# Weight preparation moved to other products of the feed-forward, query/key and shared-key stages, and three broadcasts of norm factors one product later

## The reference

```python
# end of the first block: feed-forward, then the final norm
h = rms_norm(x, norm2_g)
f = jnp.square(jax.nn.relu(h @ w_ff1))        # 1024 -> 4096
x = x + f @ w_ff2                             # 4096 -> 1024
x = rms_norm(x, final_g)
# second block, layer A
h = _rms(x, a_norm)
q, k, v, g = jnp.split(h @ a_w_in, 4, axis=-1)   # queries and keys get an own norm per head and a rotation
...                                              # differential attention
x = x + o @ a_w_out
# layer B: keys and values first
kv = _rms(x, kv_norm) @ w_kv
...                                              # stick-breaking attention, second output projection
```

## Time and profile before

| | |
|---|---|
| median of 3 runs | 2633.3 us (2632.38 to 2633.53) |
| the profiled execution | 2640.83 us, its span 2639.0 us |
| PE busy | 2385.6 us, 90% of the span |
| DVE busy | 1543.8 us, 58% |
| ACT busy | 955.1 us, 36% |
| POOL busy | 209.3 us, 8% |
| mean granted TensorE clock | 0.946 |
| DMA | 115.99 MB, mean 44 GB/s |

### The profile page before, as it was taken

How to read it: one execution, slowest core, us unless ns; L and a number is a source line. 1 busy time by engine, 2 the same in 40 slices (tenths; PEclk the granted TensorE clock), 3 DMA queues, 4 the chain that set the end, 5 groups by cost and what they waited for, 6 DMA issues and landing times.

```text
span 2639.0 us, 30077 instructions
## 1 busy us (share of the span) xinstructions
PE 2385.6 (90%) x12784; PEld 1263.2 (48%) x12784; DVE 1543.8 (58%) x1979; ACT 955.1 (36%) x1346; POOL 209.3 (8%) x264
## 2 busy tenths in 40 slices
PE   6997759999999999769999877899999998988899
PEld 3443324444444444334444445664444446776664
DVE  5579885565444555576741388975524405878852
ACT  5232233322121221323321276752212214777741
POOL 0000002000000000333310201013000000000000
PEclk9997879999999999889999989999999996889999
DMA  4010000120101101012010000012120100000021
GB/s 169 32 64 32 32 0 1 64 96 33 64 32 64 64 33 64 33 34 96 33 64 32 33 1 1 1 68 93 50 110 33 65 0 33 1 1 1 1 81 48
DMA packets 50321, 115.99 MB, mean 44 GB/s; under 512 B 2384, under 2 KB 7817, under 8 KB 49804
## 3 DMA queue, kind: packets, MB, share of 16 engines
q1 hardware_dynamic: 48452, 105.39, 11.2%
q10 hardware_dynamic: 1736, 8.68, 0.8%
HBM read 101.49 MB, written 12.58 MB: 43 GB/s over the span
## 4 chain that ended last, share of the span: by engine, by line
PE 66%; DVE 20%; ACT 8%; issue 4%; DMA 1%; POOL 1%; ACTq 0%; DVEq 0%; POOLq 0%
PE PS L72 62%; DVE R L101 7%; ACT RG L81 5%; PE PS L75 4%; DVE RG L101 2%; DVE R L93 2%; DVE mx L110 2%; DVE RG L107 2%; DVE scl L110 2%; ACT R L81 1%; ACT OV L84 1%; POOL R L93 1%; DVE RG L93 1%; DVE oss L110 0%; DVE mx L96 0%
## 5 line engine op out<-in xcount | busy, mean ns | idle before, releaser
L72 PE MATMUL PS<-R,RG 128*128 128x512 f16 (+1 forms) x5472 | 1179.2, 377 | 44.6 <-DVE R L101 29.8
L72 PEld LDWEIGHTS PS<-R,RG 128*128 128x128 f16 (+1 forms) x5472 | 545.7, 104 | 675.0 <-issue 65.7
L72 PE MATMUL PS<-RG,R 128*128 128x512 f16 x2880 | 631.6, 379 | 3.8 <-DVE R L101 3.8
L72 PEld LDWEIGHTS PS<-RG,R 128*128 128x128 f16 x2880 | 281.9, 98 | 335.7 <-DVE R L101 4.2
L81 ACT ACTIVATE R<-PS,scl 128x512 f32<-128x512 f32 (+1 forms) x200 | 131.2, 686 | 724.6 <-PE PS L72 576.7
L72 PE MATMUL PS<-R,OV 128*128 128x64 f32 (+2 forms) x1456 | 205.2, 296 | 58.2 <-DVE R L93 30.9
L101 DVE SCALAR_TENSOR_TENSOR R<-PS,scl,R 128x512 f32<-128x512 f32 (+1 forms) x216 | 154.9, 746 | 173.6 <-PE PS L72 124.9
L107 DVE TENSOR_TENSOR_SCAN RG<-RG 128x127 f32<-128x127 f32 (+7 forms) x128 | 168.6, 1345 | 120.9 <-ACT RG L81 120.5
L101 DVE SCALAR_TENSOR_TENSOR RG<-RG,scl 128x4096 f16<-128x4096 f32 x42 | 188.6, 4491 | 77.2 <-ACT RG L81 77.2
L72 PEld LDWEIGHTS PS<-R,OV 128*128 128x128 f32 x1456 | 192.1, 210 | 69.3 <-DVE R L93 37.3
L81 ACT ACTIVATE RG<-RG,scl 128x4096 f16<-128x4096 f32 x42 | 155.7, 3708 | 141.9 <-DVE scl L113 141.9
(11 more groups left out here) (109 smaller groups left out, 1536.7 us busy)
## 6 DMA issues: line engine op xcount, KB each, us to landing
RG<-in_w_ff SPq DMA_DIRECT2D x16, 2048.0 KB, 8.1
RG<-in_a_w_in SPq DMA_DIRECT2D x8, 2048.0 KB, 8.6
RG<-in_w_in SPq DMA_DIRECT2D x4, 2048.0 KB, 9.9
xspill<-R ACTq DMA_DIRECT2D x2, 4096.0 KB, 11.7
RG<-in_w_kv SPq DMA_DIRECT2D x4, 2048.0 KB, 8.4
RG<-in_b_w_in SPq DMA_DIRECT2D x4, 2048.0 KB, 7.9
R<-in_x SPq DMA_DIRECT2D x8, 512.0 KB, 9.2
RG<-in_w_out SPq DMA_DIRECT2D x2, 2048.0 KB, 7.8
```

Source lines behind the costliest of these rows:

```text
L72: return self.engine.matmul(*a, **k) if self.engine else Nothing()
```

## The change

Three things are moved; no operation is added or taken away, apart from `final_x` being issued in two halves of four k.

- Tables: tile 22 is measured at use 6 of tile 19 (before: use 1 of tile 20), with factor and high half at use 1 of tile 20 (before 2) and low half at use 2 (before 3). Tile 23 is measured at use 7 of tile 20 (before: use 1 of tile 21). Tile 24 is measured at use 2 of tile 23, u = 5 (before u = 0), converted at u = 6 and 7 (before u = 1 and 2). Tile 25 is measured at use 7 of tile 22, u = 10 (before u = 4); its conversion stays at u = 12 and 13. Tile 33 keeps its measure (use 4 of tile 31) and is converted at uses 4 and 5 of tile 32 (before: uses 5 and 6 of tile 31). Tile 34 is measured at use 8 of tile 32 and converted at uses 1 and 2 of tile 33 (before: uses 1, 2 and 3 of tile 32). Tile 35 is measured at use 5 of tile 33 and converted at uses 6 and 7 (before 1, 2 and 3).
- Half 0 of the final norm: spread at j = 8, `final_h` at j = 8 to 11, the second diagonal at j = 11, its spread at j = 12, `final_x` at j = 12 and 13.
- Half 1: the second diagonal at u = 4, its spread at u = 6, `final_x` at u = 6 and 7, the spill at u = 9.

```diff
-for _i, _at in ((21, 9), (23, 5), (35, 8)):
-    del CONVERT[_i, 2]
-    CONVERT[_i, _at] = _i + 2
-del MEASURE[35, 1]
-MEASURE[35, 3] = 37
-for _i in (7, 8, 30, 31):
+for _i in (7, 8, 19, 20, 21, 22, 23, 30, 31, 32, 33, 35):
     del MEASURE[_i, 1], CONVERT[_i, 2]
-CONVERT[6, 5] = 7
-MEASURE[7, 1], CONVERT[7, 2], MEASURE[7, 6], CONVERT[7, 7] = 8, 8, 9, 9
-MEASURE[8, 6], CONVERT[8, 8] = 10, 10
-MEASURE[30, 7], CONVERT[30, 8], MEASURE[31, 4], CONVERT[31, 5] = 32, 32, 33, 33
+
+for _j, _m, _c in ((7, None, (6, 5)), (8, (7, 1), (7, 2)), (9, (7, 6), (7, 7)), (10, (8, 6), (8, 8)),
+                   (21, (19, 1), (19, 2)), (22, (19, 6), (20, 1)), (23, (20, 7), (21, 9)),
+                   (24, (23, 2), (23, 3)), (25, (22, 7), (23, 5)), (32, (30, 7), (30, 8)),
+                   (33, (31, 4), (32, 4)), (34, (32, 8), (33, 1)), (35, (33, 5), (33, 6)),
+                   (37, (35, 3), (35, 8))):
+    CONVERT[_c] = _j
+    if _m:
+        MEASURE[_m] = _j
...
# TensorE
-                if j == 7:
+                if j == 8:
                     spread("a_norm_2", 0)
-                if j == 11:
+                if j == 12:
                     spread("final_g", 0)
...
-                if u == 5:
+                if u == 6:
                     spread("final_g", 1)
...
# VectorE
-            def final_x(n):
-                diagonal(("a_norm_2", n), ("final_g", n), 4 * n)
+            def final_x(n, ks):
...
-                if 7 <= j < 11:
-                    final_h(0, range(2 * j - 14, 2 * j - 12))
+                if 8 <= j < 12:
+                    final_h(0, range(2 * j - 16, 2 * j - 14))
                 if j == 11:
-                    final_x(0)
+                    diagonal(("a_norm_2", 0), ("final_g", 0), 0)
+                if j in (12, 13):
+                    final_x(0, range(4 * j - 48, 4 * j - 44))
...
-                if u == 5:
-                    final_x(1)
+                if u == 4:
+                    diagonal(("a_norm_2", 1), ("final_g", 1), 4)
+                if u in (6, 7):
+                    final_x(1, range(4 * u - 24, 4 * u - 20))
...
# ScalarE
-                if 7 <= j < 11:
-                    final_h(0, range(2 * j - 14, 2 * j - 12))
+                if 8 <= j < 12:
+                    final_h(0, range(2 * j - 16, 2 * j - 14))
...
-                if u == 8:
+                if u == 9:
                     spill()
```

More of the change, by code:

```diff
@@ L1329, in final_h @@
                 normalize("a_norm_2", n, XT, lambda k: SQF[n][:, k, :], ks)
-            def final_x(n):
-                diagonal(("a_norm_2", n), ("final_g", n), 4 * n)
+            def final_x(n, ks):
                 e.wait_ge(*full.at("spread", "final_g", n))
                 b = banks.ap(("spread", "final_g", n))
-                for k in range(8):
+                for k in ks:
                     x = XT[:, k, cols512(n)]
```

## The result

The changed kernel takes 2599.29 us (2594.74 to 2603.01, 4 runs), the kernel before 2633.41 us beside it (2632.38 to 2633.83, 4 runs): ratio 0.987 with an interval of 0.9853 to 0.9887. I had predicted 2597.4 us, 35.9 less; it is 34.1 less. The profiled execution of after took 2594.74 us, its span 2592.9 us.

The account below looks back on a forecast made before the run. TensorE's waits and the slow clock behind them bound the kernel; 8.6 + 22.4 - 2 + 6.9 = 35.9 us off the median 2633.3 gives 2597.4 us, range 2591 to 2609.

Parts of the forecast that it names:

- What bounds it: Whole kernel: TensorE is busy nine tenths of the span; only its idle time and matmuls at the lower clock pay.
- Part 1: Half 0 of the final norm: stall before the sums goes, the second spread's shrinks to 11.5 us; gain 8.6 us.
- Part 2: Half 1, from the first query product: both spread stalls go, u = 6 starts at 36.2 instead of 58.6; gain 22.4 us.
- Part 3: Query stage: tile 25's load meets the 4 MB spill and lands later; cost 2 us, ends 0 and 7.
- both together need at least 12 us: Part 3's step: the spill alone moves 524 GB/s, so load and spill together take at least 12 us.
- the middle: Part 3's choice for tile 25's landing: at 75 us from the first query product, costing 2 us.
- Two of my signs: Query stage: tile 25's load lands 12 to 16 us after issue; wait below 3 us at the transpose behind u = 14.
- Part 4: Shared keys' norm: the 3.29 us wait before kv_norm_2's spread and waits at z = 4 go; gain 6.9 us.
- late rotation: Rival, query stage transposes: load and spill collide fully, GpSimd's break adds waits; 7 instead of 2, another 2; 2604.4 us; chance 0.16.
- late second diagonal: Rival, half 1: spread at u = 6 waits some 8 us, 2 of slow clock; 2607.4; chance 0.12, alone or with late rotation.
- a clock that sags behind denser work: Rival, matmul stretches behind removed stalls, some 700 us: granted clock of 0.95 balances gain and loss; chance 0.02.
- a gain given back: Rival: tile 35 or 25 misses its first product and TensorE waits as long as it saved; 2633 us; chance 0.03.

Follow-up runs that it names:

- experiment 3: The changed kernel with the MEASURE and CONVERT tables put back as before; only spreads, diagonals, final_h, final_x and spill stay moved: 2619.23 us.
- experiment 4: The changed kernel with spreads, diagonals, final_h, final_x and spill (u = 8) put back as before; only the tables stay changed: 2596.71 us.
- Experiment 2: The changed kernel with the 4 MB spill issued at u = 11 instead of u = 9: 2588.34 us.
- Experiment 5: The kernel before with only the later preparation of tiles 33, 34 and 35 (shared keys and values): 2617.25 us, 14.9 below before.
- experiment 10: The kernel before run again, with no edit: 2633.82 us, ratio 0.9989 to 1.0013.

## Why the prediction was right

The total was right to 2 us and its sign for the reasons given, but not in every term: one was too small by 12.6 us, and other stages brought about as much that I had not counted. That the two cancel is luck.

- **What bounds it**: right. In the stages that the change touches, all the time came from waits of TensorE and the lower clock behind them; 7.5 us more came from the clock of a stage that it does not touch.
- **Part 1**: 8.6 said. The query products start at 1118.72 instead of 1129.05, 10.3 earlier; 1.5 of it was there before the first edited step (the last up product ends 1.5 us earlier in this execution), which leaves 8.8. The wait left over was to be 11.5 and is 12.28.
- **Part 2**: 22.4 said, 22.8 measured: u = 6 starts 35.8 us after u = 0 (1154.53 - 1118.72), before 58.6. By experiment 3 the small wait (2.58) is the tables' to remove. Of the large one (17.72) either part takes most: the order alone 15.3, the tables alone 10.7 (experiment 4 still waits 7.01).
- **Part 3, the mis-sized term**: 2 said, 14.6 measured, from u = 6 to the value products (165.9 before, 180.4 after). The collision, its place, the 13.4 us from landing to rotation (13.7 measured) and the moment at which TensorE wants it (86.3 us after u = 0 said, 86.1 measured) were right. Wrong was the landing: I took 14 us out of the range 8.6 to 17.9 and it is 20.0, above my upper end. The step that failed is "both together need at least 12 us", with "the middle" taken on it. The 12 is 6.3 MB at 524 GB/s, the spill's fastest 2 us. From issue to landing the spill alone made 341 GB/s (4.2 MB in 12.3 us), and both together 313 (6.3 MB in 20.1 us). The two landings alone added up (8.6 and 12.3 us) would have given 20.9. Two of my signs failed with it: the landing (12 to 16 us) and the wait at the transpose (below 3, measured 8.95). And I priced the first wait only; the second transpose's wait grew as well (2.42, with 6.91 us for the product behind). Experiment 2 takes 12.7 us away with one number changed, and its own stretch from u = 6 to the value products is 167.0.
- The Trainium skill ("DMA: Bandwidth & Descriptors", section "Issuing engines are not separate DMA queues") has SP's and ScalarE's transfers on the same 16 engines, interleaved. The trace agrees that they share: 20.0 us in place of 8.6. An equal share, which put the landing at 74, was too kind; it came at 81.3.
- **Part 4**: 6.9 said, 8.4 measured in after: from the start of the output projection (1729.89) to the first scores it took 427.7 us, before 436.1. Of this 3.7 are won by the sums of half 1, as said, and 4.7 behind them, where I had 3.2: before had short waits at z = 4 (1.97, 0.44, 0.34), and a granted clock of 0.76 to 0.82 from 1870 to 1878 behind the first of them, which I had not priced. Experiment 5 alone has 7.3. Tiles 33 to 36 are nowhere late.
- **What made up for part 3**: the 1.5 us ahead of the change, 1.5 more than said in part 4, 1.0 in layer A's attention and 7.5 early in the last stage (experiment 10), which the sum had at zero. 8.8 + 22.8 - 14.6 + 8.4 + 1.5 + 1.0 is 27.9, against 27.8 read at the first scores; with the 7.5 it is 35.4, and the median has 34.1. The profiled executions alone would give 18 for the last stage; some 11 of them lie where executions of one kernel differ as well (408.3 and 402.1 us in before). What gives the last stage's 7.5 us stays open: the change has no instruction there, and every edited kernel has 5.4 or more of it.
- **Rivals**: the "late rotation" was the mechanism that came true, at twice its price (14.6 for its 7), with its total (2604.4) missed by what the last stage gave. A late second diagonal, a clock that sags behind denser work and a gain given back did not occur: the mean clock rose from 0.946 to 0.955.

## What to carry to other kernels

A step that is moved moves its DMA too: before you price a stall, list for each transfer what else will be in flight in its new place, and for two at once do not take the bytes over the fastest stretch of one alone; here the sum of the two landings alone came within 1.3 us of a pair issued together (20.9 against 19.6 and 20.0, 14.9 against 14.7). A wait taken from one engine's chain ends at the next chain's own pace: here taking away 7 and then all of the 12.3 us ahead of the sums left the first scores where they were (2146.49, 2146.98 and 2148.15), and moving the sums too gave 2 us, less than the medians can show. Where a late stage runs at a clock that varies from one execution to the next, compare kernels by the start of that stage, and then look whether its first stretch differs in every execution.

## What the hardware showed that I had not expected

- A load beside a spill lands about when it would behind it: a 2 MB load takes 8.6 us alone, 14.7 beside 2 MB (6.3 alone), 19.6 and 20.0 beside 4 MB (12.3 alone) issued 0.7 us later, and 11.7 when issued 6.7 us behind a 4 MB spill (by the sum it would be 14.2). From issue to landing, read and write together moved 313 GB/s and the write alone 341.
- One GpSimd operation of 0.45 us took 4.52 us beside VectorE's whole-tile low half of 4.64, and eight additions went from 1.23 to 1.79 us each with one low half beside them, 4.5 us more in all.
- The clock granted in a stage with many short waits differs between executions of the same kernel: 0.80 and 1.00 in the same 50 us, 6.1 us on the stage. In the first 50 us of the same stage it was 0.57 and 0.58 in the two executions of before and 0.76 to 0.86 in all ten of the edited kernels.
